# A fused float32 transformer kernel on one core: a new order of splits and square roots in the attention, a float32r forget gate, and expert weights released and loaded by halves

## The reference

```python
for l in range(DEPTH):                       # first block, DEPTH = 2
    ada = silu(c) @ w_ada[l] + b_ada[l]      # six vectors: shifts, scales, gates
    h = x * (1 + sc1) + sh1
    y = mixer_ab(...) if l % 2 == 0 else mixer_cd(...)   # 16 softmax maps of 256 x 256 each
    x = layer_norm(ALPHA * x + (1 + g1) * y)
    h = x * (1 + sc2) + sh2
    x = layer_norm(ALPHA * x + (1 + g2) * swiglu(h, w_ffn_in[l], w_ffn_out[l]))
# mixer_ab: 4 heads of differential attention (two maps each, a norm over the head:
#   oa * rsqrt(mean(oa^2) + eps)), and 8 dilated heads
# mixer_cd: 8 block heads, and 8 forget heads with
#   log_f = log_sigmoid(h @ w_forget + forget_b); bias = cum(log_f)[q] - cum(log_f)[k]
...
# second block: conformer convolution, RG-LRU, then 32 experts, 2 of them for each token
y = (silu(xb @ w1[e]) * (xb @ w3[e])) @ w2[e]            # w1, w3: 1024 x 512, w2: 512 x 1024
# then a gated embedding and a last rmsnorm
```

## Time and profile before

| what | value |
|---|---|
| median of 3 runs (lowest to highest) | 1289.89 us (1289.61 to 1289.95) |
| the profiled execution | 1292.36 us, its span 1290.6 us |
| PE busy | 1218.3 us, 94% of the span |
| DVE, ACT, POOL busy | 668.8, 501.0, 54.8 us |
| bytes moved by DMA | 396 MB at a mean of 307 GB/s |
| PE's share in the chain that ended last | 69%; DMA 13%, DVE 10%, ACT 5% |

### The profile page before, as it was taken

How to read it: one execution, slowest core, us unless ns; L and a number is a source line. 1 busy time by engine, 2 the same in 40 slices (tenths; PEclk the granted TensorE clock), 3 DMA queues, 4 the chain that set the end, 5 groups by cost and what they waited for, 6 DMA issues and landing times.

```text
span 1290.6 us, 16606 instructions
## 1 busy us (share of the span) xinstructions
PE 1218.3 (94%) x6616; PEld 838.6 (65%) x6616; DVE 668.8 (52%) x1193; ACT 501.0 (39%) x744; POOL 54.8 (4%) x102
## 2 busy tenths in 40 slices
PE   6987889999999899999999999999999999999987
PEld 2686678788778877787887877544454444454436
DVE  5587968688766886774558566111111111111117
ACT  2446673343473657433445275111111111111135
POOL 0111000000000000001000300000000000000000
PEclk9998999999999999999999999999999999999999
DMA  9987667988555545777555768999999999999991
GB/s 371 391 287 226 245 240 292 271 333 322 209 190 210 208 169 216 259 264 197 193 194 204 249 245 350 394 426 427 426 427 427 394 427 427 426 427 426 425 421 41
DMA packets 48747, 396.02 MB, mean 307 GB/s; under 512 B 6225, under 2 KB 7441, under 8 KB 10418
## 3 DMA queue, kind: packets, MB, share of 16 engines
q1 hardware_dynamic: 38322, 337.69, 66.5%
q0 software_dynamic: 9568, 56.55, 12.8%
q10 hardware_dynamic: 800, 0.99, 0.2%
HBM read 391.72 MB, written 3.49 MB: 306 GB/s over the span
## 4 chain that ended last, share of the span: by engine, by line
PE 69%; DMA 13%; DVE 10%; ACT 5%; issue 3%; SPq 0%; POOL 0%; DVEq 0%; ACTq 0%
PE psum L1263 16%; PE psum L708 9%; PE psum L715 8%; PE psum L711 8%; PE psum L1302 7%; DMA slabs<-in_w 5%; DMA w_raw<-in_units 5%; PE psum L1207 4%; PE psum L1215 3%; DVE w_parts L1931 3%; DVE aring L1914 2%; DMA staged<-in_ada 2%; ACT w_parts L1389 1%; PE psum L994 1%; PE psum L1006 1%
## 5 line engine op out<-in xcount | busy, mean ns | idle before, releaser
L1931 DVE TENSOR_TENSOR w_parts<-w_raw,w_parts 128x2048 fp32r<-128x2048 f32 x106 | 242.1, 2288 | 103.1 <-ACT w_parts L1389 103.1
L1389 ACT ACTIVATE w_parts<-w_raw 128x2048 fp32r<-128x2048 f32 x106 | 202.0, 1911 | 101.2 <-DMA w_raw<-in_units 101.2
L1263 PE MATMUL psum<-slabs,arena 128*64 128x512 f32 x896 | 223.3, 593 | 4.5 <-issue 4.0
L708 PE MATMUL psum<-w_parts,h_parts 128*128 128x512 f32 x416 | 165.5, 398 | 7.6 <-DVE act_tm L2124 4.7
L711 PE MATMUL psum<-w_parts,h_parts 128*128 128x512 f32 x416 | 162.8, 391 | 0.0
L1263 PEld LDWEIGHTS psum<-slabs,arena 128*64 128x64 f32 x896 | 73.4, 137 | 113.9 <-issue 111.3
L1389 ACT ACTIVATE arena<-psum 128x512 f32<-128x512 f32 (+1 forms) x59 | 33.4, 567 | 274.7 <-PE psum L1275 141.3
L715 PE MATMUL psum<-w_parts,h_parts 128*128 128x512 f32 x416 | 112.3, 392 | 0.0
L1914 DVE CUSTOM_DVE_ANT_0 aring<-aring,cb 128x1024 f32<-128x1024 f32 x80 | 94.5, 1218 | 2.7 <-DMA aring<-in_ada 2.7
L708 PEld LDWEIGHTS psum<-w_parts,h_parts 128*128 128x128 f32 x416 | 78.4, 189 | 26.1 <-DVE act_tm L2124 6.0
L715 PEld LDWEIGHTS psum<-w_parts,h_parts 128*128 128x128 f32 x416 | 78.6, 189 | 16.8
(11 more groups left out here) (310 smaller groups left out, 1815.6 us busy)
## 6 DMA issues: line engine op xcount, KB each, us to landing
w_raw<-in_units SPq DMA_DIRECT2D x110, 1024.0 KB, 5.2
slabs<-in_w SPq DMA_DIRECT2D x32, 2048.0 KB, 18.9
slabs<-in_w SPq DMA_DIRECT2D x48, 1024.0 KB, 17.2
aring<-in_ada POOLq DMA_DIRECT2D x40, 1024.0 KB, 5.7
arena<-in_w SPq DMA_DIRECT2D x16, 2048.0 KB, 20.4
w_odd<-in_w SPq DMA_DIRECT2D x16, 2048.0 KB, 22.5
w_odd<-in_w SPq DMA_DIRECT2D x16, 1024.0 KB, 21.8
staged<-in_ada SPq DMA_DIRECT2D x8, 1024.0 KB, 16.2
```

What stands on the lines that cost most here:

```text
L708: mm(psum[:, bank, :], high(tile, tok), w_hi(k)[:, col:col + 512], start=first and bank not in begun, stop=False, skip_group_check=True)
L1263: ins = nc.tensor.matmul(psum[s * CAP:(s + 1) * CAP, w, :], xe_t[:, kt, s * CAP:(s + 1) * CAP], up_weights(w, s, b, kt), start=kt == 0, st ...
L1389: return nc.scalar.activation(out_ap, in_ap, func, **kw)
L1931: v.tensor_tensor(w_lo(k), raw(k), w_hi(k).bitcast(F32), ALU.subtract).then_inc(w_split, 1)
```

## The change

Five edits, taken together:

1. **DVE in the attention.** The split of unit QK_AT+4+pair stands inside the beat, between the shifts and `normalise`, in both layers; behind the beat stood the split of the next unit. In layer 0 at pair 3 `piece(12)` stands inside too. The split of WO_AT+2 stands behind the shifts of pair 6 in both layers (in layer 1 it stood behind pair 5).
2. **ACT in layer 0.** `head_deviation(0)` stands ahead of the exponentials of pair 3 (was behind them); `head_deviation(1)` behind `take_qk(0, 7)`, which comes later than before.
3. **Forget gate.** w_forget is split to high and low parts in float32r in layer 0's feed-forward (ACT at g = 4, DVE at g = 5), and PE does 24 float32r matmuls.
4. **Halves.** PE signals `up1_half` and `up3_half` behind tile 3 of 8. For indices 1 to 6 SP waits for a half, loads that half of the second expert's slab and of the next pair's first slab, then the other. w1 is loaded as two transfers of 1 MB everywhere. Half of w3 of pair index 1 is issued early, behind the last unit of w_out and the wait for `e_out`.
5. **Loads of index 8.** They are written out ahead of the loop: w2 stands behind `y_mm` of 7 and no longer behind up3 of 8.

```diff
+            def load_w1_half(p, s, b, i):
+                cols = slice(i * UNIT, (i + 1) * UNIT)
+                sp.dma_start(slab(0, s, b)[:, cols], a["w1"][p, s][:, cols]).then_inc(w1_loaded[s], 16)
...
             load_unit(WOUT_AT + 3)
+            sp.wait_ge(e_out, 16)
+            load_w3_half(1, 0, 1, 0)
             sp.wait_ge(unit_done, WOUT_AT + 2)
             load_w3(0, 1, 0)
...
-            sp.wait_ge(e_out, 16)
             sp.wait_ge(normed, 20)
             sp.wait_ge(ms_sum, 6)
-            load_w3(1, 0, 1)
+            load_w3_half(1, 0, 1, 1)
...
             for n in range(1, AHEAD):
                 b = n % 2
-                sp.wait_ge(up1, n)
-                load_w1(n, 1, b)
-                load_w1(n + 1, 0, 1 - b)
-                sp.wait_ge(up3, n)
-                load_w3(n, 1, b)
-                load_w3(n + 1, 0, 1 - b)
+                for i in range(2):
+                    sp.wait_ge((up1_half, up1)[i], (up1_half_from, 0)[i] + n)
+                    load_w1_half(n, 1, b, i)
+                    load_w1_half(n + 1, 0, 1 - b, i)
+                for i in range(2):
+                    sp.wait_ge((up3_half, up3)[i], (up3_half_from, 0)[i] + n)
+                    load_w3_half(n, 1, b, i)
+                    load_w3_half(n + 1, 0, 1 - b, i)
...
             load_ups(AHEAD, AHEAD, AHEAD % 2)
-            with sp.Fori((AHEAD + 1) // 2, PAIRS // 2) as i:
+            n = AHEAD + 1
+            load_w1(n, 0, 0)
+            for c in range(2):
+                sp.wait_ge(y_mm[c], AHEAD)
+                load_w2(n, 0, c)
+            sp.wait_ge(up1, n)
+            load_w1(n, 1, 0)
+            load_w3(n, 0, 0)
+            sp.wait_ge(up3, n)
+            load_w3(n, 1, 0)
+            load_pair(n + 1, n + 1, 1)
+            with sp.Fori(n // 2 + 1, PAIRS // 2) as i:
...
-                    pe.wait_ge(later_in, LATER)
-                    for part in (h_hi, h_lo):
+                    pe.wait_ge(forget_split, forget_split_from + 2)
+                    for n, (w, part) in enumerate(((w_forget_hi, h_hi), (w_forget_lo, h_hi), (w_forget_hi, h_lo))):
                         for kt in range(KT):
-                            ins = mm(psum[0:8, 4, 0:T], w_forget[:, kt, :], part[:, kt, :].bitcast(F32),
-                                     start=kt == 0 and part is h_hi, stop=kt == KT - 1 and part is h_lo)
+                            ins = mm(psum[0:8, 4, 0:T], w[:, kt, :], part[:, kt, :], start=n == 0 and kt == 0,
+                                     stop=n == 2 and kt == KT - 1)
...
-                    pe.wait_ge(w1_loaded[s], m * 16)
+                    pe.wait_ge(w1_loaded[s], m * 32)
...
+                        if kt == 3:
+                            ins.then_inc((up1_half, up3_half)[w], 1)
...
+                if layer == 0 and pair == 3:
+                    head_deviation(0)
                 exps(layer, 2 * pair)
...
-                if layer == 0 and pair in (3, 5):
-                    head_deviation(pair // 4)
...
                     take_qk(layer, j)
+                    if layer == 0 and j == 7:
+                        head_deviation(1)
                     split(u + QK_AT + j + 3)
...
+                split(LAYER_UNITS * layer + QK_AT + 4 + pair)
+                if layer == 0 and pair == 3:
+                    piece(9 + pair)
                 for i in items_of(layer, pair):
                     normalise(layer, i)
...
                 for j in range(2):
-                    split(u + QK_AT + j + 3)
+                    if j == 0:
+                        split(u + QK_AT + 3)
...
-                    if layer == 0 or pair:
-                        piece((9, 37)[layer] + pair)
                     if layer == 0 and pair == 3:
                         gate_col(0)
-                    if layer == 0 and pair in (3, 5):
-                        scale_heads(pair // 4)
-                    if layer or pair < 5:
-                        split(u + QK_AT + 2 + pair + 3)
+                        scale_heads(0)
+                    elif layer == 0 or pair:
+                        piece((9, 37)[layer] + pair)
+                    if layer == 0 and pair == 5:
+                        scale_heads(1)
...
                 if layer == 0:
                     heads_low(1)
-                    split(u + WO_AT + 2)
+                split(u + WO_AT + 2)
```

More of the change, by code:

```diff
@@ L1316, in _ @@
             n_all = rounds * PAIRS
-            pair(n_all, 1, rounds * (PAIRS // 2), True)
+            pair(n_all, 1, rounds * (PAIRS // 2), last=True)
             second_products(1, rounds * (PAIRS // 2 * 16))
@@ L1642, in _ @@
                     split(k + 5)
+                    if layer == 0 and g == 4:
+                        act.wait_ge(later_in, LATER)
+                        A(w_forget_hi[:], w_forget[:], Cp).then_inc(forget_split, 1)
                     gate(layer, g, 0)
@@ L2285, in _ @@
                         forget_constants((g - 5) // 2)
+                    if layer == 0 and g == 5:
+                        dve.wait_ge(forget_split, forget_split_from + 1)
+                        v.tensor_tensor(w_forget_lo[:], w_forget[:], w_forget_hi[:].bitcast(F32),
+                                        ALU.subtract).then_inc(forget_split, 1)
                     if layer == 0 and at_ == 24:
```

14 lines of the change are left out of this document (11 added, 3 removed).

## The result

The changed kernel takes 1271.46 us (median of 4 runs, 1269.56 to 1273.76) beside 1289.75 us of the kernel before (4 runs, 1289.48 to 1289.95): a ratio of 0.9859, 95% interval 0.9842 to 0.9876, 18.3 us less. On another chip, further down, the same two kernels gave 1269.34 beside 1290.70 us, a ratio of 0.9836 (0.9815 to 0.9857), 21.4 us less. The first difference is 16.0 to 20.4 us by its interval, the second 18.5 to 23.9, so the two agree within their noise. 1268 was forecast, within 1263 to 1277. The ratio is not quite that of the two medians. Where the experiments give a ratio and then a gain in us, the gain is worked out from the ratio, and is up to 1.3 us off the difference of the medians. The profiled execution took 1273.76 us, its span 1272.0; that of before 1292.36 and 1290.6, so the two traces differ by 18.6 us.

The account below looks back on a forecast made before the run. TensorE was taken to bound the experts, with DMA also full, and VectorE to set the first attention's beat. Savings 8.1 + 4.1 + 6.0 + 4.2 = 22.4 us from 1289.9 gave 1267.5, rounded to 1268; range 1263 to 1277.

Parts of the forecast that it names:

- the band of the forecast: Whole kernel: the time expected if the summed gains hold, 1265 to 1271 us, chance 0.55.
- E: Expert loads: each of 32 more w1 transfers costs a fixed 0.1 us, 3.2 us in all; 1270.7 us, chance 0.05.
- B: Experts: earlier releases gain nothing as transfers share one stream; 1271.7 us, chance 0.08.
- Layer 0, beats 0 to 2: First attention, first three pairs of maps: split fills VectorE's 1.75 us wait; each pair falls to 7.6 us.
- Layer 0, the whole: First layer's attention: reordered VectorE and ScalarE work saves 8.1 us, bounds 5 and 9.5.
- beat 3: First attention, pair 3: split and piece(12) cover ScalarE's table load back and exponentials; 10.66 us becomes 9.1.
- beats 4 and 5: First attention, pairs 4 and 5: VectorE waits 2 to 3 us for scores; pair 6's shift comes at about 120.4.
- The gap on PE at the third joint output: First attention: TensorE waits about 4 us for scale_heads(0), in place of 3.40 + 2.05 us.
- Forget gate: Second layer's forget matmuls: 24 in float32r replace 32 float32 passes, 7.00 to 2.9 us, saving 4.1; lower bound 1.7.
- Layer 1: Second layer's attention: split after the shift removes TensorE's waits and half-clock stretch, saving 6.0 us; bounds 2 and 7.
- Experts: Expert weight loads: earlier releases shrink DMA's idle gaps and TensorE's waits, saving 4.2 us; bounds 1 and 5.5.
- The start of the arithmetic: Experts in the kernel before: modelled TensorE waits at pairs 7, 8, 14, 15 and 16 total 6.9 us.

## Why the prediction was right, and where it wasn't

- **The time.** 21.9 us less than the median were forecast (1268); 18.3 us were measured on the first chip, whose interval (16.0 to 20.4 us) leaves the forecast out, and 21.4 on another, whose interval (18.5 to 23.9 us of 1290.70) has it in. Faster was right, and both times lie in the range; the first is 0.5 us outside the band of the forecast (1265 to 1271), at the time of rivals E (1270.7) and B (1271.7). Of E something came true, as told below; B, by which the experts give nothing, did not, since they give 1.5 us. Part of the hit is luck: in the pair of traces a gain of 2.8 us that nobody forecast and a loss of 3.2 us at the start of the experts nearly cancel.
- **Layer 0, beats 0 to 2: right.** Beat 7.6, measured 7.56 us; the wait ahead of normalise is gone. At the shift of pair 3 DVE is 7.3 us ahead, 6.8 were forecast.
- **Layer 0, the whole: 8.1 forecast, 6.6 in the first trace, about 7 over all.** Six traces with the new order start the feed-forward at 154.6 to 156.4 us (mean 155.4; the one with piece(12) moved, at 157.7, apart), seven with the old one at 160.9 to 163.9 (mean 162.5).
  - The step that was mis-sized most is beat 3: it takes 10.43 us (88.88 to 99.31) where 9.1 was forecast and 10.66 stood before. I wrote that split and piece(12), 4.7 us of work, cover the two table loads, and did not ask whether the transfer of piece(12) had landed. It waits 0.50 to 1.75 us in the six traces with piece(12) in that place, 1.50 in the first; with 0.50 the beat takes 9.43 us.
  - The transfer is issued when piece(10) is done, which the faster beat moves by 3.3 us, to 81.7. Yet it lands at 93.8 us, where it landed at 94.0 before: 12.1 us from issue, and not 9.0. It shares the DMA with SP's units, busy to 0.81 of the stage (0.77 before); what holds it up in there is not shown. For piece(15) the same wait was in the sum, since the trace of before showed it; for piece(12) it didn't show, and I left it out.
  - Another 0.6 us goes in beats 4 and 5, 22.4 us together where the sum has 21.8. The wait for PE's scores was forecast (2 to 3 us; 2.14 came). The gap on PE at the third joint output is 4.96 us in place of some 4.
  - The order of the two table loads and their 1.28 us each were right: the square root came 1.30 us after its load began, and the exponentials 1.30 us after theirs. So the 2.7 us more that I had estimated from the Trainium skill (ScalarE: Activation LUTs, section What ACT_TABLE_LOAD costs) did not come.
- **Forget gate: 4.1, measured 4.3.** 24 matmuls in 2.80 us; 8 stationary columns go at the pace of 128.
- **Layer 1: 6.0, measured 5.8.** With the forget gate 10.1 forecast and 10.0 measured; the stage takes 97.0 us in all six traces. `from_heads` came 16.8 us sooner and not 18.4; the difference is layer 0's.
- **Experts: 4.2 forecast, 1.5 measured. This is the step that failed.** 430.4 to 430.8 us from the first to the last w1/w3 matmul in five traces with the old loads, 428.5 to 429.9 in four with the new ones (2.2 us less in the pair of traces of before and after). The releases did what was said: the dip of 1012 is gone, and in the first trace PE waits at pairs 15 and 16 alone, 0.60 + 0.31 + 1.50 + 0.32 = 2.7 us (in two other traces pair 7 waits as well, 0.77 and 1.39 us). 2.7 is the figure of the sum, and still the gain is a third to a half of what was forecast. Two things were mis-sized:
  - The price of the halves, which I took at nothing. Rival E had it, with 0.05 for a chance and 0.1 us for each w1 transfer more, 3.2 us in all; 0.075 us is what was measured, 0.15 us a pair, 2.4 us over 16 pairs, though it hangs on the rows and not, as E has it, on the transfer. With w1 whole but for the first release the waits left are 1.7 and 2.5 us, and the stretch is 427.5 and 428.1 us.
  - The start of the arithmetic. It gave the kernel before 6.9 us of waits; its trace has 1.41 at pair 8, 1.27 + 0.31 at 15 and 1.35 + 0.34 at 16, 4.7 in all (by the spacings of the pairs, against PE's own 27.42 us, 5.6 us before and 3.5 after). I had the larger of these beside me and let the 6.9 stand. So even with the price nearly gone the two traces with w1 whole reach 2.7 and 3.3 us of the 4.2.
  - The rows that should have warned me of the price are the earlier trace rows: I saw that four 1 MB and four 2 MB transfers left no room between them, and took that for a sign that a transfer costs nothing but its bytes. It only says that the price isn't idle time of the DMA. The packets of that same trace, 614.8 and 313.7 ns, would have given it.
  - The Trainium skill (DMA: Bandwidth & Descriptors, section Anatomy of one DMA — SWDGE (gpsimd) path; estimate 1332 us) gives its 2.0 us for a transfer that GpSimd issues; these are SP's. No such part showed up: 32 more transfers cost 2.4 us and not 64.
  - A small slip: the further issues on SP are 32 (300 and 268 in the traces), not 38.
- **The clock, not forecast.** PE's granted clock at the start of the experts took 3.2 us of the gain in the first trace and none in the next, with the same kernel. Whether it makes the spread between 18.3 and 21.4 us isn't shown: the other executions have no trace, and the two intervals overlap.
- **The second feed-forward and what follows it, not forecast.** In the pair of traces it is 2.8 us less from the end of the second projection to the end of the last unit ahead of routing. 1.8 us of that is one wait in the trace of before, whose cause is a unit that lands late on ACT:

```profile
605.49 1.92 ACT L1389 ACTIVATE w_parts<-w_raw 128x2048 fp32r<-128x2048 f32 x1 [7.42 <-DMA w_raw<-in_units]
...
610.12 0.50 PE L708 MATMUL psum<-w_parts,h_parts 128*128 128x512 f32 x1 [1.78 <-DVE act_tm L2124]
```

It is there, 0.42 to 1.78 us long, in five of the eight traces in which one layer or both had the old order, and in none of the six with the new order in both. Which transfer is in its way is open; that the change moves the meeting of two transfers is a guess.
- **Sum by stages, from the two traces of before and after:** 6.6 (layer 0) + 0.2 + 10.0 (layer 1 and gate) + 2.8 - 3.2 (clock at routing) + 2.2 (experts) = 18.6 us, as much as between the spans.

## What to carry to other kernels

Put independent work into a wait that another engine's latency makes, and it is free, but follow every load that the faster beat will ask for earlier: here one transfer made a wait of 1.5 us, and moving its user only moved the wait to the next two. Where the DMA stream is the bound, shorter rows are paid for in every transfer, so cut a transfer only where the earlier release closes a gap (the traces speak for it, the times can't tell). When an arithmetic gives more waits for the kernel before than its trace has, mend it before taking differences. A change of 1% is judged by stages of the trace when the clock moves the whole time by as much as the effect.

## What the hardware showed

- In a saturated DMA stream the rate goes with the length of the rows: from 1050 to 1150 us 426 GB/s with w1 in rows of 16 KB, 424 with 8 KB, 415 with w1 and w3 in quarters (rows of 4 KB), each packet more costing 0.5 to 0.7 ns of the stream.
- Transfers to 64 partitions ran at half the rate of those to 128: 20.2 us for 4 MB in place of 9.8, with the DMA engines busy all the while (one run).
- A wait of 1.85 us on PE was followed by 3.4 us at half its clock, in one trace. The stretch at half clock at the start of the experts was 10.2 and 3.4 us long in two traces of one and the same kernel, and 0, 3.4 or 6.8 us in the others.
- float32r matmuls with 8 stationary columns and 256 moving ones follow each other in 0.117 us (24 in 2.80 us), as those with 128 columns do.
